# SGU values turned token-major step by step, and restarts behind a norm taken set by set over both weight halves

## The reference, cut to what matters

```python
def modulate(x, g, shift, scale):
    return rms_norm(x, g) * (1.0 + scale[:, None, :]) + shift[:, None, :]

def sgu_mixer(zu, zv, w_sp, b_sp, ln_g, ln_b):        # 1024 channels, 4 groups, chunks of 128 tokens
    u = jax.nn.gelu(zu)
    v = layer_norm(jax.nn.gelu(zv), ln_g, ln_b)
    w = jnp.where(tril, w_sp, 0.0)[:, :L, :L]
    mixed = jnp.einsum('gts,bnsgc->bntgc', w, v.reshape(B, n, L, SGU_GROUPS, SGU_GD))
    mixed = mixed + b_sp[:, :L].T[:, :, None]
    return u * mixed.reshape(B, T, D_SGU), v

def mix_cd(z, ...):
    yc, v_rows = sgu_mixer(zu, zv, sgu_w, sgu_b, sgu_ln_g, sgu_ln_b)
    yd = swa_banded(q, k, v, att_sinks)               # prompt; swa_buffered for the samples
    return jnp.concatenate([yc, yd], axis=-1), v_rows, ...
```

## Time and profile before

| | |
|---|---|
| median of three runs | 2903.96 us (2903.19 to 2906.1) |
| the profiled execution | 2900.26 us, of which the span from its first to its last instruction is 2898.3 |
| busy | PE 2741.6, DVE 1402.5, ACT 1149.1, POOL 87.8 us |
| the chain that ended last | PE 87%, DVE 4%, DMA 4%, ACT 3%, issue 1% |
| mean granted TensorE clock | 0.957 of 2.4 GHz |
| DMA | 603.57 MB, mean 208 GB/s |

### The profile page before, as it was taken

The page is one execution under the profiler, slowest core; times in us unless marked ns, Lnnn a source line. Parts: engine busy times, 40 slices in busy tenths (PEclk is TensorE's granted clock), DMA queues, the critical chain, the costliest instruction groups (busy, mean ns, idle before and its releaser), DMA issues.

```text
span 2898.3 us, 47711 instructions
## 1 busy us (share of the span) xinstructions
PE 2741.6 (95%) x20153; PEld 2520.2 (87%) x20153; DVE 1402.5 (48%) x1845; ACT 1149.1 (40%) x1429; POOL 87.8 (3%) x116
## 2 busy tenths in 40 slices
PE   5899997989999999999999899798999999999998
PEld 1698875878888888898999799688999999999998
DVE  1599856343444333344444556435545444454444
ACT  2333254343344322334343446424444423444443
POOL 1000010000000000000000000101000000000000
PEclk7899986999999999999999999779999999999999
DMA  9667783766777688777634433224344344444443
GB/s 386 273 253 291 277 200 97 292 233 262 281 276 276 262 317 329 282 277 287 233 141 167 163 139 144 73 93 170 120 170 168 132 160 178 174 163 155 147 160 132
DMA packets 75774, 603.57 MB, mean 208 GB/s; under 512 B 21029, under 2 KB 22373, under 8 KB 24050
## 3 DMA queue, kind: packets, MB, share of 16 engines
q1 hardware_dynamic: 75634, 601.54, 56.2%
HBM read 592.01 MB, written 9.49 MB: 208 GB/s over the span
## 4 chain that ended last, share of the span: by engine, by line
PE 87%; DVE 4%; DMA 4%; ACT 3%; issue 1%; SPq 0%; POOL 0%; DVEq 0%; POOLq 0%; ACTq 0%
PE ps L654 26%; PE ps L656 25%; PE ps L655 25%; PE ps L784 5%; DMA pre_ring<-in_w_ada 3%; DMA aring<-in_w_ada 1%; DVE w_lo L1437 1%; ACT w_hi L1087 1%; PE ps L797 0%; DVE cacc L1532 0%; DVE act_lo L1635 0%; PE ps L769 0%; ACT tn L1250 0%; DVE tn L1616 0%; PE ps L1017 0%
## 5 line engine op out<-in xcount | busy, mean ns | idle before, releaser
L1437 DVE TENSOR_TENSOR w_lo<-raw,w_hi 128x2048 fp32r<-128x2048 f32 (+1 forms) x402 | 835.7, 2080 | 1112.6 <-ACT w_hi L1087 1112.4
L654 PE MATMUL ps<-act_hi,w_hi 128*128 128x288 f32 x4320 | 1294.3, 300 | 43.3 <-DVE act_lo L1635 31.4
L655 PE MATMUL ps<-act_hi,w_lo 128*128 128x288 f32 x4320 | 1279.0, 296 | 0.0
L656 PE MATMUL ps<-act_lo,w_hi 128*128 128x288 f32 x4320 | 1274.3, 295 | 0.0
L1087 ACT ACTIVATE w_hi<-raw 128x2048 fp32r<-128x2048 f32 (+1 forms) x402 | 699.3, 1741 | 1086.3 <-PE ps L656 1074.9
L654 PEld LDWEIGHTS ps<-act_hi,w_hi 128*128 128x128 f32 x4320 | 814.0, 188 | 104.4 <-issue 94.9
L656 PEld LDWEIGHTS ps<-act_lo,w_hi 128*128 128x128 f32 x4320 | 817.4, 189 | 0.0
L655 PEld LDWEIGHTS ps<-act_hi,w_lo 128*128 128x128 f32 x4320 | 815.4, 189 | 0.1
L654 PE MATMUL ps<-hid_hi,w_hi 128*128 128x288 f32 x1408 | 420.6, 299 | 8.6 <-DVE w_lo L1437 8.6
L655 PE MATMUL ps<-hid_hi,w_lo 128*128 128x288 f32 x1408 | 417.0, 296 | 0.0
L656 PE MATMUL ps<-hid_lo,w_hi 128*128 128x288 f32 x1408 | 415.5, 295 | 0.0
(11 more groups left out here) (271 smaller groups left out, 1429.9 us busy)
## 6 DMA issues: line engine op xcount, KB each, us to landing
aring<-in_w_ada SPq DMA_DIRECT2D x176, 1024.0 KB, 8.0
raw<-in_w_gu SPq DMA_DIRECT2D x88, 2048.0 KB, 8.1
raw<-in_w_dn SPq DMA_DIRECT2D x64, 1408.0 KB, 6.0
raw<-in_w_ab SPq DMA_DIRECT2D x20, 2048.0 KB, 8.1
raw<-in_w_out SPq DMA_DIRECT2D x16, 2048.0 KB, 8.2
raw<-in_w_cd SPq DMA_DIRECT2D x13, 2048.0 KB, 8.1
pre_ring<-in_w_ada SPq DMA_DIRECT2D x16, 1024.0 KB, 10.2
aring<-in_state_glaT SPq DMA_DIRECT2D x4, 1024.0 KB, 7.4
```

Source lines behind the costliest of these rows:

```text
L654: pe.matmul(bank, w_hi[:, h, cols], hi[:, kt, :], start=begin, stop=False)
L655: pe.matmul(bank, w_lo[:, h, cols], hi[:, kt, :], start=False, stop=False)
L656: mm = pe.matmul(bank, w_hi[:, h, cols], lo[:, kt, :], start=False, stop=end)
L1437: dve.tensor_tensor(w_lo[:, h, 0:w], raw[:, par, h * w:(h + 1) * w], w_hi[:, h, 0:w].bitcast(F32), ALU.subtract).then_inc(split_done, 1)
```

## The change

**Restart.** Behind the norms 1 to 3 the 16 tiles pass in five sets of 2, 4, 4, 4 and 2. PE's new `restart` takes both weight halves for each set before it waits for the next one; the conditioning pair of that step goes ahead of it. The last square of a norm is no longer added by POOL but by PE, as a second product with ones. The second half of the first step's weights is split in two parts, one ahead of and one behind the last epilogue, and `amod` is made there too. The first half of the second step is split in two parts (6 and 10 tiles), and PE starts it on the first part.

**SGU.** In each sgu step PE turns the v tile of the step before to token-major (`turn_values`, the last in `mix1`), ACT copies it, DVE takes its statistics per token. In `mix1` DVE takes the mean off and applies the gain, spread earlier over all rows (`g_low`, `g_high`); the reciprocal root goes into the mixing weights, which ACT scales (`sc_ring` holds them then); the bias of the layer norm and that of the mixing go in as one product of two rows each (`biases`), for which a load brings the layer norm bias as one row, element by element. The sample rows for the output are turned back after the first output step. `sc_ring` keeps three tiles, `ptp` one.

**Other.** `then_wait` no longer holds for gu followed by down, nor for sgu. SP waits for `rows_set`, a memset behind the norm, ahead of the constants.

```diff
@@ the plan
-        _a.then_wait = not isinstance(_b, Seg) or "down" in (_a.kind, _b.kind)
+        _a.then_wait = _a.kind != "sgu" and (not isinstance(_b, Seg) or _a.kind == "down")
...
+PE_SQUARES = [39, 55, 71, 87]
+SETS = [(0, 2), (2, 6), (6, 10), (10, 14), (14, 16)]
+EARLY = 6
@@ SyncE
-                        sp.wait_ge(act_ready, 4 * KT)
...
+                        sp.wait_ge(rows_set, 1)
...
+                        sp.dma_start(mix_b[64:65, :].rearrange("a (j p) -> a j p", p=P),
+                                     t["vec"][:, bj:bj + CT].rearrange("p j -> j p").unsqueeze(0), allow_slow_non_contiguous=True) \
+                            .then_inc(mix1_consts, 16)
@@ TensorE
+            def turn_values(j):
+                pe.wait_ge(drained, SGU_SEG.n0 + j + 1)
+                pe.wait_ge(pt_ready, 6 + j if j < CT - 1 else len(ATT))
+                for c in range(2):
+                    pe.transpose(ps[:, 6, c * P:(c + 1) * P], zv[:, j % 2, c * P:(c + 1) * P], ident[:])
+                pe.transpose(ps[0:32, 6, 256:384], zv[:, j % 2, NP_TOK:T], ident[:]).then_inc(zv_turned, 1)
...
+            def restart(n, par):
+                pe.wait_ge(drained, n - 1)
+                for k0, k1 in SETS:
+                    pe.wait_ge(act_ready, sets[0] * KT + k1)
+                    for h in range(2):
+                        bank = ps[:, 2 * par + h, 0:T]
+                        if k0 == 0:
+                            pe.wait_ge(split_done, n * 2 + (h + 1))
+                        for kt in range(k0, k1):
...
+                        if k1 == EARLY and h == 0:
+                            mm.then_inc(part_done, 1)
+                        if k1 == KT:
+                            mm.then_inc(half_done, 1)
...
+                mm = pe.matmul(ps[:, STAT_BANK, 0:T], ones[:], ssq[:], start=True, stop=not split)
+                if split:
+                    pe.wait_ge(sq_ready, last + 1)
+                    mm = pe.matmul(ps[:, STAT_BANK, 0:T], ones[:], square_of(last), start=False, stop=True)
...
             def mix1(after):
...
+                att_point(len(ATT) + 1)
+                pe.wait_ge(scored, len(ATT))
+                biases(0)
+                turn_values(CT - 1)
+                att_point(len(ATT) + 2)
+                biases(1)
+                mixing(0)
+                mixing(1)
                 pe.wait_ge(act_ready, sets[0] * KT + CT)
                 for h in range(2):
                     pe.wait_ge(split_done, after.n0 * 2 + h + 1)
                     out_part(after.n0, after.n0 % 2, h, range(CT, KT))
...
+                biases(2)
+                mixing(2)
+                pe.wait_ge(sgu_mixed, 1)
+                biases(3)
+                mixing(3)
@@ ScalarE, in a step
+                    if nxt and end and seg.norm_next:
+                        act.wait_ge(half_done, n * 2 + 2)
+                        high_part(nxt, n + 1, 1 - par, 1, 0, CT).then_inc(first_hi, 1)
+                    if seg.kind == "sgu":
+                        if ls:
+                            values_to_rows(ls - 1)
+                        else:
+                            weight_rows()
...
                     epilogue(seg, n, par, ls)
...
+                    if nxt and end and seg.norm_next:
+                        high_part(nxt, n + 1, 1 - par, 1, CT, KT).then_inc(hi_done, 1)
+                    elif nxt and hurry and not seg.mixed_next:
@@ VectorE
+            def value_stats(j):
+                dve.wait_ge(zv_ready, j + 1)
+                cols = slice(j * P, (j + 1) * P)
+                dve.bn_stats(tile_stats[:, 0, j, :], vt0[:, cols])
+                dve.bn_stats(tile_stats[:, 1, j, :], vt1[:, cols])
+                return dve.bn_stats(tile_stats[0:32, 2, j, :], vts[:, cols])
...
                 elif seg.kind == "sgu":
...
+                    if ls >= 2:
+                        dve.wait_ge(zv_turned, ls - 1)
+                    dve.tensor_tensor(zv[:, ls % 2], b1, sg[:, 1], ALU.mult).then_inc(drained, 1)
```

More of the change, by code:

```diff
@@ L115 @@
         _gel += _s.steps
-        _q += CT
     if _s.kind == "z":
@@ L141, with sets_of, set_no, taken_by_pe @@
 Q_SEG = next(s for s in SEGS if s.kind == "q")
+OUT1 = next(s for s in SEGS if s.kind == "out" and s.layer)
 SGU_SEG = next(s for s in SEGS if s.kind == "sgu")
 Z_SEG = next(s for s in SEGS if s.kind == "z")
-SQUARES = [0, 16, 24, 40, 56, 64, 80, 96]
-NORM_STATS = [1, 3, 4, 6, 7]
+SQUARES = [0, 16, 24, 40, 56, 72, 88]
+PE_SQUARES = [39, 55, 71, 87]
+NORM_STATS = [1, 3, 4, 5, 6]
+SETS = [(0, 2), (2, 6), (6, 10), (10, 14), (14, 16)]
+EARLY = 6
 Y_PARTS = [slice(0, 2), slice(2, 4), slice(4, 8), slice(8, 12), slice(12, 14), slice(14, 16)]
 GLA_A = 4 * PRE + 2 * MIX_PAIRS
+def sets_of(k):
+    return SETS if k else [(4 * g, 4 * g + 4) for g in range(4)]
+def set_no(k, g):
+    return (4 + len(SETS) * (k - 1) if k else 0) + g
+def taken_by_pe(q):
+    return sum(q > last for last in PE_SQUARES)
 def lin(i, per, c):
@@ L424, in build, with g_of, mix_bank @@
         ATT_OUT = ps[:, 7, 0:256]
+        ROWS = slice(64, 66)
+        vts = mix_a[0:32, 0:CT * P]
+        wsp_s = mix_b[0:32, 0:P].rearrange("p (g t) -> p g t", t=32)
+        wsp_sr = mix_b[0:32, P:2 * P]
+        turn_s = mix_b[0:32, 2 * P:2 * P + 32]
+        v_out = qs[:].rearrange("p b r t -> p b (r t)")
+        def g_of(tiles):
+            half = g_high if tiles.start >= CT // 2 else g_low
+            return half[:, tiles.start % 4 * P:(tiles.stop - 1) % 4 * P + P]
+        def mix_bank(g):
+            return (4, 2 * (1 - OUT1.n0 % 2), 6, 4)[g]
         geb_of = [free_lo[:, j * T:(j + 1) * T] for j in (KT - 4, KT - 2)]
@@ L598, in sum_squares @@
             def sum_squares(n, q):
-                for k in range(n):
+                for k in range(n - (q + n - 1 in PE_SQUARES)):
                     pool.wait_ge(sq_ready, q + k + 1)
@@ new lines, in turn_values, with biases @@
+            def turn_values(j):
[4 more added lines that the diff above has]
+                pe.transpose(ps[0:32, 6, 256:384], zv[:, j % 2, NP_TOK:T], ident[:]).then_inc(zv_turned, 1)
+            def biases(g):
+                for b in range(2):
+                    mm = pe.matmul(ps[:, mix_bank(g) + b, 0:T], mix_b[ROWS, (2 * g + b) * P:(2 * g + b + 1) * P],
+                                   mix_a[ROWS, g * T:(g + 1) * T], start=True, stop=False)
+                mm.then_inc(bias_set, 1)
@@ new lines, in mixing @@
+            def mixing(g):
+                pe.wait_ge(vn_ready, g + 1)
+                pe.wait_ge(wr_ready, 1)
+                pe.wait_ge(bias_set, g + 1)
+                for b in range(2):
+                    bank = ps[:, mix_bank(g) + b, 0:T]
+                    vs = slice((2 * g + b) * P, (2 * g + b + 1) * P)
+                    for c, vt in enumerate((vt0, vt1)):
+                        pe.matmul(bank[:, c * P:(c + 1) * P], vt[:, vs], sc_ring[:, c, g * P:(g + 1) * P], start=False, stop=False)
+                    mm = pe.matmul(bank[:, NP_TOK:T], vts[:, vs], wsp_sr[:, 32 * g:32 * g + 32], start=False, stop=True)
+                mm.then_inc(mixed_ready, 1)
@@ L838, in body @@
                         out_part(n, par, 1, range(CT))
+                        turn_samples()
+                        continue
+                    if first and n in RESTARTS:
+                        if p is not None:
+                            ada_pair(p)
+                        restart(n, par)
                         continue
@@ L983, in mix1 @@
             def mix1(after):
-                for p in range(len(ATT) + 1, len(ATT) + 3):
-                    att_point(p)
-                pe.wait_ge(drained, SGU_SEG.n0 + SGU_SEG.steps)
-                for j in range(CT):
-                    mm = pe.matmul(ps[:, MEAN_BANK, 0:T], ones[:], zv[:, j, :], start=(j == 0), stop=(j == CT - 1))
-                mm.then_inc(mean_ready, 1)
+                att_point(len(ATT) + 1)
[6 more added lines that the diff above has]
+                mixing(1)
                 pe.wait_ge(act_ready, sets[0] * KT + CT)
@@ L1238, in norm @@
                 if not final:
-                    for g in range(4):
+                    for g in range(len(SETS)):
                         norm_group(k, g)
```

389 lines of the change are left out of this document (254 added, 135 removed).

## The result

| | before | after |
|---|---|---|
| median, us | 2904.97 (2903.19 to 2906.1, 4 runs) | 2841.47 (2839.35 to 2843.5, 4 runs) |
| the profiled execution, us | 2900.26 | 2843.5 |
| mean granted clock, of 2.4 GHz | 0.957 | 0.967 |

The ratio is 0.9782, with a 95% interval of 0.9765 to 0.9799: faster by 63.5 us, 2.2%. The forecast was 2849.0, so 7.5 us too slow, within its range. Between the two profiled executions the saving is 56.8 us; the forecast's sum was 55.0. One execution of the last kernel tried (e12) took 5273.55 us, for a reason that nothing here shows; the ratio there leaves it out.

A forecast was written before the change was run, and what follows sets the result against it. TensorE, busy for 95% of the span, was taken as the bound. Savings of 8.9 + 1.1 + 6.0 + 1.0 + 29.5 + 8.5 = 55.0 us gave 2845.3, or 2849 on the median's scale; range 2830 to 2872.

The forecast's parts named there:

- The bound and the places: TensorE bounds the kernel; savings lie in three norm restarts, the mix stage and about four short waits.
- Part 1: Restarts behind norms 1 to 3: earlier sums and sets save 8.9, 6.6 and 6.0 us; last norm 1.0.
- the sum of squares: At the norms: PE adds the last square, sum about 1 us earlier, 0 to 0.9 behind output segments.
- The stall: Behind norm 2: weights queued behind a four-byte-element load arrive late, 3.5 us stall plus 2 at half clock.
- Rival (d): Four-byte load behind norm 2 runs on one DMA engine: 51.7 us ahead of the weights, total 2897.5; 5%.
- Rival (c): Four-byte load behind norm 2 runs on eight engines: twice 3.2 us, 3.2 more stall, total 2852; 25%.
- Part 2: Token-major values: mix stage 34.8 us shorter, less 5.3 paid on PE, so 29.5 net.
- Rival (e): Mix stage: attention tail and ACT's chain set the end, stage near 65 instead of 54.5, total 2860; 8%.
- Part 3: Four gate/up to down transitions: the second half is no longer split late, saving PE waits of 8.5 us.
- The scale: Whole kernel: 3.7 us added because the three-run median, 2903.96, stood above the profiled execution.
- (a): Clock stays up through the mix stage: 12.5 us better, total 2836; 10%.
- (b): Clock stays down through the restarts: three times 8.1 us worse, total 2873; 10%.

The follow-up runs named there:

- e12: Changed kernel with query weights loaded first and two mix-stage moves, plus PE summing the last two squares behind both output segments: 2831.26 us.
- e4: Changed kernel, but POOL adds the last square of every norm again and PE sums once: 2849.58 us.
- e2: Changed kernel with the element-by-element layer norm bias load replaced by one contiguous row of another input, same queue place: 2837.81 us.
- e8: Changed kernel with the first output step's second weight half split behind the last u/v epilogue and two bias products ahead of the sample values: 2841.32 us.
- e3: Kernel before with one line changed, so gate/up followed by down no longer splits its second half late: 2886.87 us.
- e7: Changed kernel with 20 unread matmuls in PE's wait for the first sample values in the mix stage: 2844.09 us.
- e11: Changed kernel with query weights loaded first, two mix-stage moves and recounted, mostly fewer unread matmuls in PE's waits at the restarts: 2831.9 us.
- e6: Changed kernel with unread matmuls in PE's waits ahead of and behind the sum of norms 1 to 3: 2845.5 us.
- e9: Changed kernel run again unaltered, as the base for later runs: 2842.09 us.

## Why the prediction was right, and where it was not

**The bound and the places** were right: apart from 1.6 us lost at the start, the change in time lies at the places that the forecast named, and the steps between them run at the same pace in both traces.

**Part 1** was right in its shape. From the end of the first normalising (1620.18) to the end of the step it is 18.2 us, as worked out (18.3), and the first set's first matmul stands 3.2 us in (3.25). That normalising in the kernel after:

```profile
1619.43 0.75 DVE L1829 TENSOR_TENSOR tn<-x,rstd 128x576 f32<-128x576 f32 x1
```

What failed is the sum of squares: the forecast let norm 3 gain up to 0.9 there and norm 1 as much. In fact POOL's remaining addition lay beside the moved subtraction and took 1.7 us, and PE's two products then ran at half clock, so that at norm 3 the root was ready 6.6 us behind the last matmul, against 5.4 before. The last step of the root there, in the kernel after (last matmul 1971.38) and before (2013.95):

```profile
1977.51 0.44 ACT L1256 ACTIVATE rstd<-rstd 128x288 f32<-128x288 f32 x1
...
2018.89 0.44 ACT L1098 ACTIVATE rstd<-rstd 128x288 f32<-128x288 f32 x1
```

That is the 1.5 us missing at norm 3, and part of the 1.8 at norm 1 (e4, e12): of the 8.9 there only 7.9 follow from the forecast's own terms (6.0 as at norm 3, and 1.9). The rest was put down to a clock that rises earlier. It did, it was up from the first matmul on, and the step took 14.8 us as at the other two. At norm 2, where no addition is left, 7.0 against 6.6.

**The stall** was 5.9 us against 5.5 (4.6 of wait and 1.3 of half clock, against 3.5 and 2), by the mechanism named, and the small packets cost 4.4 in place of 3.2. The row behind the 3.2 is SyncE's time to issue eight stores; the load here was issued in 0.85, and slowed the two issues behind it and the way of the weights instead (e2). Rival (d) is out, at 51.7. Rival (c), by the rule of the Trainium skill's "DMA: Bandwidth & Descriptors", section "Why a DMA increments its semaphore by 16 and not by 1", had 6.4. The trace lists no engines, and 4.4 lies between 3.2 and 6.4, nearer to the forecast's. What was held up behind the packets was more than eight engines: from 1641 to 1645 us the sixteen were busy for 0.91 of the time while they moved 55 GB/s, where in e2 they moved 418 from 1638 to 1640. On how many the load itself ran stays open.

**Part 2** was the largest term and held step by step. From the last u/v matmul: the sample values start at 6.1 (forecast 6.3) and end at 11.6 (12.0), the first mixings end and the output product starts at 30.4 (31.2). Behind that point it is 25.5 us against 21.7 and 1.5 for the clock, since the clock fell once more in the last mixings and was still at half for the first matmuls of the other half (0.84 and 0.78 in the rows above). The cost in the q and u/v steps was 5.1 against 5.3, and the epilogue hides behind PE as said. Rival (e) is out, and e8 shows that what stands ahead of the sample values counts in full.

**Part 3** was the mis-sized term: 8.5 forecast, 16.3 measured. The step that failed took the wait alone for the price of the wait. It left out the half clock behind it at two places, and at the first it looked only at what covers PE, not at what the late split holds back on SyncE's queue (e3).

**The scale** failed as well. The sum stood against one execution of 2900.26, and I moved it by the 3.7 us to the median. The kernel after had its own profiled execution 2.0 us above its median. So of the 7.5 us by which the forecast was too high, 3.7 are this step, 2.0 that execution, and 1.8 the terms, in which 7.8 too little in part 3 is set against some 6 us too much elsewhere (norms 1 and 3, the mix stage, and 1.6 lost where nothing was changed). That the number came out this near is in part luck: these errors cancel.

**Rivals (a) and (b).** The clock did not stay up in the mix stage, and the fillers of e7 kept it up only through the first sample values. It rose within the restarts, behind norm 2 of the kernel after with the second set; before the third set it would not have mattered (e11), later it would (e4, e6).

## What to carry to other kernels

A wait of PE costs the wait, what may run at half clock behind it, and what the late engine holds back on the DMA queue: look at the pitch of the matmuls behind it and at the next loads before pricing it. Before an operation is moved next to a GpSimd addition, look at what VectorE reads there; and before a constant load goes ahead of weights, count its packets, or send the weights first. Terms of 2 to 5 us in a kernel of 2.8 ms are read stage by stage from the same instructions of two traces, for the whole differs by as much from one run to the next.

## What the runs showed that I had not expected

- A 128x288 float32 addition on GpSimd takes 0.8 us alone and 1.5 to 2.5 beside VectorE's subtraction of two SBUF inputs, by how much of that is left (e4, norm 3 above).
- Behind the 1024 four-byte packets the DMA does not come back at once. The packets themselves are recorded within some 2 us, and then the caches, queued behind them, move at 37 GB/s for a while, where in e2, without the burst, it was 418 (1638 to 1640 us). Two windows of the DMA view of the kernel after, 1640 to 1642 and 1642 to 1644 us:

```profile
DMA packets 887, 0.19 MB, mean 96 GB/s; under 512 B 841, under 2 KB 841, under 8 KB 887
...
DMA packets 18, 0.07 MB, mean 37 GB/s; under 512 B 0, under 2 KB 0, under 8 KB 18
```

- TensorE's clock fell to half in the mix stage in the midst of products that left no gap (e7), and the same kernel had it at 0.84 in one execution and at 0.69 in another over the same 48 matmuls and two mixings (e9).
